# The second block's norms by token and the convolution's first tap on ScalarE, in a two-block fp32 kernel

## The chip, the cores and the metric

The kernel runs on one core of one Trainium2 chip, as one program. The metric is the device time of one execution in microseconds, over several runs; one further execution was taken with the hardware profiler, and all durations below are from it. Engines: PE is TensorE (its records of weight loads are PEld), DVE is VectorE, ACT is ScalarE, POOL is GpSimd, SP is SyncE.

## The reference, cut to what matters

Two blocks run on 256 tokens of width 2048, in fp32. The change is in the second one. Its input projection gives, for every token, q and k (12 heads each) and v (24 heads) of 128 columns, a gate z, and the queries of a cross attention. What the change touches is how these are made ready:

```python
def rms_norm(x, g):
    xf = x.astype(jnp.float32)
    y = xf * lax.rsqrt(jnp.mean(xf * xf, axis=-1, keepdims=True) + EPS)
    return (y * g.astype(jnp.float32)).astype(x.dtype)

def l2_norm(x):
    return (xf * lax.rsqrt(jnp.sum(xf * xf, axis=-1, keepdims=True) + EPS)).astype(x.dtype)
...
    qkv = jax.nn.silu(causal_depthwise_conv(p[..., :c_qkv], conv_w))      # DN_CONV = 4 taps
    q = l2_norm(q heads), k = l2_norm(k heads)                            # 24 heads of 128
...
    q = rms_norm(xq.reshape(B, S, XA_HEADS, XA_DIM), qn_g)                # cross attention: 4 heads of 256
    k = rms_norm(kv[..., :XA_WIDTH].reshape(B, -1, XA_HEADS, XA_DIM), kn_g)
```

## The kernel before

Data lie with features on the 128 partitions and the 256 tokens in the free dimension. The second block projects 88 tiles of 128 columns: eight for the cross attention's queries, then 40 pairs of tiles, numbered q from 0, that are q and k (pairs 0 to 11), v and z. A pair is seven groups of eight 128x128x128 products (one Strassen step), 56 in all; an fp32 product stands in the trace as two records. PE issues all of them from one line (L2263, in `halves`), and they are the filler of everything else in the block: `plan` lists the places of the program and how much filler goes behind each (a unit there is 7/4 products), and `fill(name)` issues it. The places that matter are n0 and n1 ahead of the cross attention, s, t and o of its four heads, j3, j4 and v0 behind it, and then six groups g0 to g5 of the recurrence. PE, ACT and DVE each run their own queue in order; ACT and DVE put their part of the pairs where `keeps_by`, `firsts_by` and `seconds_by` say, which compare a pair's groups with the filler's positions.

For each pair ACT copies two banks out after the second group (`keep`, L2503). DVE makes two sums behind the fourth group (`first`, L2720 and L2722) and the next pair's weight sums (L2702 to L2705), and the last sums behind the seventh group (`second`, L2733). Then `conv` runs the four taps of two tiles on DVE: the first as a product with a column (L2751), three as multiply-adds (L2754); ACT applies silu (L2510) into `A2`. The products of pair q wait for `first` of pair q-1 at their first group, for `second` of pair q-1 at the third, and for `keep` of pair q at the fifth.

There are five norms n = 0 to 4: n = 0 for the memory's keys, n = 1 for the cross attention's queries (groups of two tiles), n = 2, 3, 4 for eight tiles of q and k each. Each has four steps. ACT squares eight tiles (`norm_squares`, L2529). PE sums over the partitions with a matrix of ones as the stationary operand (`norm_sums`, L2288), which leaves the sum of each token and head on all 128 partitions. ACT takes the root of that (`norm_roots`, L2537), 128x1024 for n = 0 and 1, 128x2048 for the others. DVE takes the inverse of the same size (L2784) and multiplies (`norm_scale`, L2787, or L2790 with a gain). In DVE's queue the inverse of norms 1, 3 and 4 stands ahead of a `first`, and that of norm 2 ahead of the fourth head's row maxima.

Of the kernel before, what the change touches and what calls it, by code (L numbers as in the profile page):

```python
# [21 lines left out]
ALU = mybir.AluOpType  # L22
# [77 lines left out]
def build(nc, a, out):  # L100
# [30 lines left out]
    with outer:  # L131
# [1930 lines left out]
        tmpa, keep2 = x_f[0:VH, 0:TX], x_f[0:VH, TX:2 * TX]  # L2062
        sqj = o_f[:, 0:2048].rearrange("p (t n) -> p t n", n=TX)
# [57 lines left out]
        with phase() as c:  # L2121
            (x1_ready, x1_out, x1_back, group_done, kept, paired, xsums, tsums, hin, ab_done, ab_out, tile_done, conv_chain, silu_done, z_silu, gated, xq_taken,
             squares, summed, roots, inverse, normed, bchain, gchain, dchain2, mchain, ttr, tout, s_done, mx, e_done, rcp,
# [6 lines left out]
                "z_silu", "gated", "xq_taken", "qk_squares", "qk_summed", "qk_roots", "qk_inverse", "qk_normed",  # L2130
# [7 lines left out]
            with nc.Block() as block:  # L2138
# [81 lines left out]
                def _(pe):  # L2220
# [59 lines left out]

                    def norm_sums(n):
                        per = norm_jobs[n][1]
                        pe.wait_ge(squares, n + 1)
                        if n:
                            pe.wait_ge(roots, n)
# [28 lines left out]
                    norm_sums(1)  # L2314
                    fill("n1")
                    for h in range(XH):
# [12 lines left out]
                        if h == 2:  # L2329
                            norm_sums(2)  # L2330
# [17 lines left out]
                        fill(f"o{h}")  # L2348
                    fill("j3")
                    norm_sums(3)  # L2350
                    fill("j4")
                    norm_sums(4)
                    fill("v0")
                    for i in range(NG):
                        if i == 0:
                            pe.wait_ge(roots, 5)
                            pe.wait_ge(xo_out, XH)
# [124 lines left out]
                def _(act):  # L2482
                    at = [0]
# [21 lines left out]
                    def silu(q):  # L2505
                        kind, _, dst, had = pair_tiles(q)
                        to = pair_to[:, q % 2, :, :]
                        if kind == "c":
                            act.wait_ge(conv_chain, DCONV * (had + 2))
# [5 lines left out]
                    def pairs_to(upto, whole=False):  # L2515

                        for q in range(at[0], upto):
                            keep(q)
                            if q:
                                silu(q - 1)  # L2520
                            at[0] = q + 1

                    def drain(name, then):
                        pairs_to(keeps_by(name, then))
# [6 lines left out]
                    def norm_roots(n):  # L2531
# [51 lines left out]
                    drain("n0", "n1")  # L2583
                    norm_roots(1)
                    drain("n1", "s0")
                    for h in range(XH):
# [5 lines left out]
                        drain(f"s{h}", f"t{h}")  # L2592
                        act.wait_ge(pt_done, h + 1)
# [11 lines left out]
                        if h == 2:  # L2605
                            norm_roots(2)
# [5 lines left out]
                    drain("j4", "v0")  # L2612
# [8 lines left out]
                    drain("v0", "g0a")  # L2621
# [50 lines left out]
                    pairs_to(NQ)  # L2672
# [3 lines left out]
                def _(dve):  # L2676
# [63 lines left out]
                    def conv(q):  # L2740
                        _, wt, _, had = pair_tiles(q)
                        if had >= 4:
                            dve.wait_ge(silu_done, had - 2)
                        dve.wait_ge(paired, 4 * q + 4)
                        for d in range(DCONV):
                            for j in range(2):
# [3 lines left out]
                                if d == 0:  # L2750
                                    ins = nc.vector.tensor_scalar(to, src, tap, None, ALU.mult)  # L2751
                                else:
                                    dve.wait_ge(conv_chain, DCONV * had + 2 * (d - 1) + j + 1)
                                    ins = nc.vector.scalar_tensor_tensor(to[:, d:], src[:, 0:TX - d], tap, to[:, d:],  # L2754
                                                                         ALU.mult, ALU.add)
                                ins.then_inc(conv_chain, 1)
# [22 lines left out]

                    def norm_scale(n):  # L2780
                        x, per, _, gain = norm_jobs[n]
                        w = 8 // per
                        dve.wait_ge(roots, n + 1)
                        nc.vector.reciprocal(rtj[:, 0:w, :], rtj[:, 0:w, :]).then_inc(inverse, 1)  # L2784
                        dve.wait_ge(inverse, n + 1)
                        if gain is None:
                            nc.vector.tensor_tensor(x, x, rtj[:, :, :], ALU.mult).then_inc(normed, 1)  # L2787
                        else:
                            for t in range(8):
                                nc.vector.scalar_tensor_tensor(x[:, t, :], x[:, t, :], pcol(gain, t % 2), rtj[:, t // 2, :],  # L2790
                                                               ALU.mult, ALU.mult).then_inc(normed, 1)
# [11 lines left out]
                    for m in range(MT):  # L2803
                        nc.vector.tensor_scalar(x1[:, m, :], y_tok[:, m, :], ssf[:, SCALE1, m:m + 1], None, ALU.mult).then_inc(x1_ready, 1)
                    norm_scale(0)
# [15 lines left out]
                    drain("n0", "n1")  # L2821
# [237 lines left out]
```

## Time and profile before

| what | us |
|---|---|
| median of 3 runs | 3817.94 |
| lowest and highest | 3814.05, 3818.92 |
| the profiled execution's own time | 3816.08 |
| its span | 3814.4 |
| in it, the first product of pair 0 to the end of v0 | 301.5 of the span |
| in it, the recurrence and the last filler | 600.9 of the span |

The span begins with the first instruction of the profile and ends with the last; some 1.7 us of the execution lie around it. The page's first section gives busy times over the whole span, but the block that the change is in covers less than a third of it, so the rows of the section below are of that block's stretches. An idle time in a row is put down to the instruction that released the engine. PEclk is the share of TensorE's full clock that was granted in a stretch.

### The profile page before, as it was taken

The page shows a single profiled execution, that of the slowest core. Times are in us where ns is not written, and L with a number is a line of the kernel's source. Part 1 is how long each engine was busy: PE and PEld are TensorE (multiplying, and loading weights), DVE is VectorE, ACT ScalarE, POOL GpSimd, SP SyncE. Part 2 cuts the span into 40 slices and gives each one's busy share as a digit, 9 for nine tenths or more (in the row PEclk, how much of TensorE's full clock was granted, in tenths as well). Part 3 has the DMA queues.
Part 4 walks back from the last instruction along what each step waited for, and adds up shares of the span by engine and source line. Part 5 has one row for each costly group of instructions (what it writes and reads, how often), then busy time and mean ns, then how long its engine had stood idle before and what let it go on. Part 6 is the DMA issues. An engine that isn't in the chain of part 4 may idle for free. (4 is left out here: it accounts for less than half of the span.)

```text
span 3814.4 us, 50735 instructions
## 1 busy us (share of the span) xinstructions
PE 3604.1 (94%) x20578; PEld 3176.4 (83%) x20578; DVE 2113.4 (55%) x4109; ACT 626.1 (16%) x1423; POOL 927.4 (24%) x813
## 2 busy tenths in 40 slices
PE   8999999999999999998778999999878899999899
PEld 6878887899988888887667777776878899999888
DVE  5882102255520789655787444445366867666554
ACT  0002112100011122220446000002121122222100
POOL 0001000101000344546776545453000121122000
PEclk9999999999999999999999999999989999999999
DMA  5434332344544799997994999997323322221342
GB/s 211 143 130 144 144 122 78 122 177 168 219 188 167 262 364 385 385 388 241 313 316 175 347 334 330 346 336 265 122 101 132 111 95 95 95 95 67 129 192 111
DMA packets 159013, 776.64 MB, mean 204 GB/s; under 512 B 19476, under 2 KB 21420, under 8 KB 122812
## 3 DMA queue, kind: packets, MB, share of 16 engines
q1 hardware_dynamic: 100536, 518.52, 37.2%
q0 software_dynamic: 57344, 251.69, 18.0%
q10 hardware_dynamic: 900, 3.17, 0.3%
q8 instruction: 164, 2.69, 0.3%
q14 instruction: 69, 0.57, 0.0%
HBM read 762.67 MB, written 10.64 MB: 203 GB/s over the span
## 5 line engine op out<-in xcount | busy, mean ns | idle before, releaser
L405 PE MATMUL PS<-mem,ring 128*128 128x272 f32 (+1 forms) x2816 | 647.7, 393 | 3.0 <-DMA ring<-in_first_tiles 3.0
L405 PEld LDWEIGHTS PS<-mem,ring 128*128 128x128 f32 x2816 | 541.6, 193 | 106.9 <-issue 4.6
L1272 POOL DMA_INDIRECT mem<-in_peer_ug,idx x256 | 313.0, 1223 | 639.7 <-DVE idx L1786 347.1
L1839 DVE CUSTOM_DVE_ANT_0 mem<-mem 128x1152 f32<-128x1152 f32 x256 | 349.0, 1365 | 137.4 <-DMA mem<-in_peer_ug,idx 131.2
L1924 DVE SCALAR_TENSOR_TENSOR mem<-mem 128x768 f32<-128x768 f32 x256 | 261.3, 1021 | 288.0 <-DMA mem<-in_peer_vg,idx 282.1
L1386 PE MATMUL PS<-mem 128*128 128x256 f32 x1792 | 387.5, 379 | 1.4 <-DMA mem<-in_peer_ud 1.4
L2263 PE MATMUL PS<-mem,ring 128*128 128x128 f32 x2560 | 328.1, 283 | 60.8 <-DVE mem L2722 42.4
L1386 PEld LDWEIGHTS PS<-mem 128*128 128x128 f32 x1792 | 340.2, 190 | 48.3 <-DMA mem<-in_peer_ud 2.2
L2263 PEld LDWEIGHTS PS<-mem,ring 128*128 128x128 f32 x2560 | 312.4, 199 | 64.3 <-issue 45.0
L413 PEld LDWEIGHTS PS<-mem,ring 128*128 128x128 f32 x3136 | 350.3, 192 | 0.1
L413 PE MATMUL PS<-mem,ring 128*128 128x128 f32 x3136 | 350.3, 275 | 0.0
L1298 POOL DMA_INDIRECT mem<-in_peer_vg,idx x256 | 278.7, 1089 | 280.4 <-DVE mem L1924 224.2
L2216 POOL TENSOR_TENSOR mem<-mem,ring 128x512 f32<-128x512 f32 x84 | 114.2, 1376 | 769.8 <-DVE mem L2874 573.4
L1462 PE MATMUL PS<-mem,ring 128*128 128x512 f32 (+1 forms) x768 | 297.4, 523 | 2.1 <-DMA mem<-in_peer_vd 2.1
L1462 PE MATMUL PS<-mem 128*128 128x512 f32 (+1 forms) x768 | 296.2, 523 | 0.0
L1462 PEld LDWEIGHTS PS<-mem,ring 128*128 128x128 f32 x768 | 217.9, 298 | 71.0 <-DMA mem<-in_peer_vd 2.7
L1462 PEld LDWEIGHTS PS<-mem 128*128 128x128 f32 x768 | 217.7, 298 | 68.4
L2263 PE MATMUL PS<-mem 128*128 128x128 f32 x1920 | 240.4, 278 | 11.9 <-DVE ring L2733 11.9
L2263 PEld LDWEIGHTS PS<-mem 128*128 128x128 f32 x1920 | 228.4, 194 | 13.4 <-DVE ring L2733 13.0
L934 DVE SCALAR_TENSOR_TENSOR mem<-mem 128x256 f32<-128x256 f32 x480 | 191.7, 473 | 0.0
L1425 PE MATMUL PS<-mem 128*128 128x256 f32 x512 | 131.5, 403 | 44.6 <-DMA mem<-in_mem_w_kv 43.6
L1425 PEld LDWEIGHTS PS<-mem 128*128 128x128 f32 x512 | 97.2, 200 | 65.4 <-DMA mem<-in_mem_w_kv 47.4
(407 smaller groups left out, 4414.4 us busy)
## 6 DMA issues: line engine op xcount, KB each, us to landing
ring<-in_first_tiles SPq DMA_DIRECT2D x144, 1024.0 KB, 4.8
ring<-in_dn_tiles SPq DMA_DIRECT2D x88, 1024.0 KB, 4.9
mem<-in_peer_vd SPq DMA_DIRECT2D x128, 640.0 KB, 7.0
mem<-in_peer_ud SPq DMA_DIRECT2D x128, 448.0 KB, 6.6
ring<-in_out_panels SPq DMA_DIRECT2D x16, 2048.0 KB, 8.5
ring<-in_w_out SPq DMA_DIRECT2D x8, 2048.0 KB, 8.9
ring<-in_peer_wq SPq DMA_DIRECT2D x8, 2048.0 KB, 8.0
mem<-second_keys SPq DMA_DIRECT2D x64, 256.0 KB, 5.3
```

Of the source, the lines that this page charges most:

```text
L405: last = nc.tensor.matmul(PS[:, 4 + n % 4, 0:T if wide else TX], wslots[slot_of[n]][:, k, :], x, start=(k == 0), stop=(k == KT - 1))
L413: last = nc.tensor.matmul(PS[:, bank, at * P:(at + 1) * P], w[:, k, :], x[:, k, :], start=(k == 0), stop=(k == KH2 - 1))
L934: ins = nc.vector.scalar_tensor_tensor(dst, src, w, acc[:, j % 4, :], ALU.mult, ALU.add)
L1272: nc.gpsimd.indirect_dma_start(Ug[:, at % US, :], None, a["peer_ug"], bass.IndirectOffsetOnAxis(ap=idx[:, n, j:j + 1], axis=0)).then_inc(u ...
L1298: nc.gpsimd.indirect_dma_start(Vg[:, at % GS, :], None, a["peer_vg"], bass.IndirectOffsetOnAxis(ap=idx[:, n, j:j + 1], axis=0)).then_inc(v ...
L1386: last = nc.tensor.matmul(PS[:, i % BANKS_U, 0:TX], Ut[i % UT][:, k * P:(k + 1) * P], xnD[:, k, :], start=(k == 0), stop=(k == KU - 1))
L1425: last = nc.tensor.matmul(PS[:, KVB[side], 0:PW], x, y, start=(k == 0), stop=(k == KT - 1))
L1462: last = nc.tensor.matmul(to, weights_of[m][:, i // LO, :, i % LO], Vd[:, i % VS, at:at + w], start=(i == 0), stop=(i == NKEY - 1))
L1839: nc.vector.tensor_tensor_reduce(out=Ug[:, at % US, :], in0=Ug[:, at % US, :], in1=h_tok[:, m, CU:D], scale=1.0, scalar=0.0, op0=ALU.mult, ...
L1924: nc.vector.scalar_tensor_tensor(hc, Vg[:, at % GS, :], dots[:, m, h * PTOP + j:h * PTOP + j + 1], hc, ALU.mult, ALU.add).then_inc(vg_used, 1)
L2216: nc.gpsimd.tensor_tensor(No[:, m, :, :], NT_[:, m, :, :], lev[:, l:l + 1, :].broadcast_to([P, VG, P]), ALU.mult).then_inc(no_ready, 1)
L2263: ins = nc.tensor.matmul(to, w[:, k, :], y[:, k, :], start=(k == 0 and group in (0, 2, 3)), stop=(k == GROUP - 1), skip_group_check=True)
```

## The change

Norms 1 to 4 no longer put each token's sum on all partitions. `token_sums` makes the squares the stationary operand and one column of ones the moving one, so the sums of a norm stand as 128 tokens by 8 or 16 columns. Root (ACT) and inverse (DVE, the new `norm_inverse`) work on that small tile, `per_token`. `spread_inverse` brings the inverses back to all partitions with 8 or 16 products against the identity, into four PSUM banks, and DVE multiplies from there. The filler is divided so that a norm's sums, inverse and spread stand apart, and 16 units of it move from v0 to n1. In `conv` the first tap is left out; ACT makes it as a copy scaled by a column (`first_tap`) behind a pair's last sums, and DVE's remaining three taps wait for it (`tapped`). Norm 0, the other matrices and all data are as before.

```diff
-        plan = [("x0", 128), ("n0", 24), ("n1", 40)]
+        plan = [("x0", 128), ("n0", 24), ("n1a", 8), ("n1b", 20), ("n1c", 28)]
...
-        plan += [("j3", 24), ("j4", 120), ("v0", 112)]
+        plan += [("j3", 24), ("j4a", 8), ("j4b", 24), ("j4c", 88), ("v0a", 8), ("v0b", 24), ("v0c", 64)]
...
+        per_token = o_f[:, 2048:2064]
+        spread_of = PS[:, 0:4, :].rearrange("p b (t n) -> p (b t) n", n=TX)
...
+                    def token_sums(n):
...
+                        for g in range(8 // per):
+                            for m in range(MT):
+                                for e in range(per):
+                                    last = nc.tensor.matmul(PS[:, 0, g * MT + m:g * MT + m + 1],
+                                                            sqj[:, g * per + e, m * P:(m + 1) * P], ones[:, 0:1],
+                                                            start=(e == 0), stop=(e == per - 1))
...
+                    def spread_inverse(n):
...
+                        pe.wait_ge(inverse, n + 1)
+                        for g in range(8 // per):
+                            for m in range(MT):
+                                c = g * MT + m
+                                last = nc.tensor.matmul(spread_of[:, g, m * P:(m + 1) * P],
+                                                        per_token[:, c:c + 1].broadcast_to([P, P]), ident[:, :],
+                                                        start=True, stop=True)
...
-                    norm_sums(1)
-                    fill("n1")
+                    token_sums(1)
+                    fill("n1a")
+                    fill("n1b")
+                    spread_inverse(1)
+                    fill("n1c")
...
-                            norm_sums(2)
+                            token_sums(2)
...
                         fill(f"o{h}")
+                        if h == 2:
+                            spread_inverse(2)
...
+                    def first_tap(q):
...
+                            act.wait_ge(paired, 4 * q + 4)
+                            for j in range(2):
+                                tap = PD * (CQKV // P) + wt + j
+                                nc.scalar.activation(dacc[:, had % 4 + j, :], pair_to[:, q % 2, 2 * j:2 * j + 2, :].rearrange("p b n -> p (b n)"),
+                                                     ACT.Copy, scale=dcw[:, tap:tap + 1]).then_inc(tapped, 1)
...
-                        nc.scalar.activation(rtj[:, 0:w, :], PS[:, 0:w // 2, :].rearrange("p b (t n) -> p (b t) n", n=TX),
-                                             ACT.Sqrt, bias=eps_c[:, :], scale=scale).then_inc(roots, 1)
+                            nc.scalar.activation(per_token[:, 0:MT * w], PS[:, 0, 0:MT * w], ACT.Sqrt, bias=eps_c[:, :],
+                                                 scale=scale).then_inc(roots, 1)
...
-                        for d in range(DCONV):
+                        for d in range(1, DCONV):
...
+                                if d == 1:
+                                    dve.wait_ge(tapped, had + j + 1)
...
                         if gain is None:
-                            nc.vector.tensor_tensor(x, x, rtj[:, :, :], ALU.mult).then_inc(normed, 1)
+                            nc.vector.tensor_tensor(x, x, by, ALU.mult).then_inc(normed, 1)
```

In the orders below L2265 is the line of the pairs' products after the change (L2263 before). PE's queue around norm 3 before, with the sums on all partitions as L2288:

```order
L2263 MATMUL PS<-mem 128x128 x2
L2288 MATMUL PS<-mem,ones 128x256 x8
L2263 MATMUL PS<-mem 128x128 x6
L2263 MATMUL PS<-mem,ring 128x128 x24
L2263 MATMUL PS<-mem 128x128 x16
```

PE's queue around norm 3 after, with `token_sums` as L2294 and `spread_inverse` as L2306; pair 10 begins with the last 14 of the 22 products ahead of L2306:

```order
L2265 MATMUL PS<-mem,ring 128x128 x22
L2294 MATMUL PS<-ones,mem 128x1 x16
L2265 MATMUL PS<-mem,ring 128x128 x2
L2265 MATMUL PS<-mem 128x128 x16
L2265 MATMUL PS<-mem,ring 128x128 x8
L2265 MATMUL PS<-mem 128x128 x8
L2265 MATMUL PS<-mem,ring 128x128 x22
L2306 MATMUL PS<-ident,mem 128x128 x16
L2265 MATMUL PS<-mem,ring 128x128 x2
L2265 MATMUL PS<-mem 128x128 x16
```

The sums move half a pair later, and the spread stands 56 products behind them and two products ahead of the third group of pair 10.

DVE's queue at the same norm before: inverse and multiplication stand directly ahead of a `first`.

```order
L2754 SCALAR_TENSOR_TENSOR ring<-ring,dcw 128x253 x2
L2784 RECIPROCAL mem<-mem 128x2048
L2787 TENSOR_TENSOR mem<-mem 128x2048
L2720 TENSOR_TENSOR mem<-PS,mem 128x128
L2722 TENSOR_TENSOR mem<-PS,mem 128x128
L2702 TENSOR_TENSOR mem<-ring 128x1024
```

DVE's queue there after, with the inverse as L2839, the multiplication as L2849, `first` as L2778 and L2780, `second` as L2791:

```order
L2839 RECIPROCAL mem<-mem 128x16
L2778 TENSOR_TENSOR mem<-PS,mem 128x128
L2780 TENSOR_TENSOR mem<-PS,mem 128x128
L2760 TENSOR_TENSOR mem<-ring 128x1024
L2761 TENSOR_TENSOR ring<-ring 128x1024
L2763 TENSOR_TENSOR mem<-ring,mem 128x1024
L2784 TENSOR_TENSOR ring<-mem 128x128
L2849 TENSOR_TENSOR mem<-mem,PS 128x2048
L2791 TENSOR_TENSOR ring<-PS,mem 128x384
```

The inverse is now ahead of `first` of pair 9 and the multiplication between it and `second` of pair 9. At norm 4 the multiplication stands directly behind the inverse and ahead of `first` of pair 13; at norm 2 both stand ahead of the fourth head's row maxima, as before.

ACT's queue at norm 3 after, with the squares as L2581, the root as L2589, the first taps as L2560 and `keep` as L2542; before, a `keep` came directly behind the root:

```order
L2581 ACTIVATE mem<-mem 128x2048
L2589 ACT_TABLE_LOAD
L2589 ACTIVATE mem<-PS,eps_c 128x16
L2560 ACTIVATE ring<-ring,dcw 128x256 x2
L2542 ACTIVATE mem<-PS 128x2x128
L2549 ACT_TABLE_LOAD
```

The first taps of pair 8 now wait behind the root of norm 3, and the `keep` of pair 9 behind them.

## Rows read from the trace of the kernel before

**Rows 1.** Windows: stretch, its length, busy us (records) of PE PEld DVE ACT POOL, PEclk, DMA.

```profile
2711.70:3013.20 301.50, 243.60 (x1938) 238.01 (x1939) 200.39 (x298) 64.20 (x90) 0.00 (x0) 0.90 0.31 113
3013.20:3614.10 600.90, 565.87 (x4909) 559.21 (x4907) 397.75 (x599) 144.03 (x234) 114.19 (x84) 0.99 0.25 91
```

**Rows 2.** Waits of PE from 2711 to 3014.9: us in total, times, longest.

```profile
PE PS L2263 <- DVE mem L2722: 38.9, 5, 14.9
PE PS L2263 <- ACT mem L2503: 17.6, 2, 15.9
PE PS L2288 <- ACT mem L2529: 1.1, 1, 1.1
```

**Rows 3.** Timeline of PE at norm 3: start, us, line, records, idle time before.

```profile
2882.34 3.62 PE L2288 MATMUL PS<-mem,ones 128*128 128x256 f32 x16
...
2903.95 6.41 PE L2263 MATMUL PS<-mem,ring 128*128 128x128 f32 x32 [14.87 <-DVE mem L2722]
2910.19 3.74 PE L2263 MATMUL PS<-mem 128*128 128x128 f32 x32
```

**Rows 4.** Timeline of DVE at norm 2.

```profile
2832.72 12.95 DVE L2784 RECIPROCAL mem<-mem 128x2048 f32<-128x2048 f32 x1 [8.08 <-ACT mem L2537]
2845.71 2.29 DVE L2787 TENSOR_TENSOR mem<-mem 128x2048 f32<-128x2048 f32 x1
2847.91 0.42 DVE L2828 TENSOR_REDUCE mem<-PS 128x1 f32<-128x256 f32 x1
...
2848.89 0.15 DVE L2830 TENSOR_SCALAR mem<-mem 128x1 f32<-128x1 f32 x1
2850.40 0.29 DVE L2720 TENSOR_TENSOR mem<-PS,mem 128x128 f32<-128x128 f32 x1 [1.36 <-ACT mem L2503]
```

**Rows 5.** Timeline of PE at its other waits in this stretch.

```profile
2736.54 6.48 PE L2263 MATMUL PS<-mem,ring 128*128 128x128 f32 x32 [8.58 <-DVE mem L2722]
...
2755.55 2.02 PE L2263 MATMUL PS<-mem,ring 128*128 128x128 f32 x16 [1.86 <-DVE mem L2722]
...
2776.98 1.89 PE L2324 MATMUL PS<-mem 128*128 128x256 f32 x8
2778.71 1.05 PE L2263 MATMUL PS<-mem 128*128 128x128 f32 x8
2781.42 2.05 PE L2263 MATMUL PS<-mem,ring 128*128 128x128 f32 x16 [1.66 <-ACT mem L2503]
...
2805.64 5.46 PE L2263 MATMUL PS<-mem,ring 128*128 128x128 f32 x32 [1.86 <-DVE mem L2722]
...
2850.42 3.78 PE L2263 MATMUL PS<-mem,ring 128*128 128x128 f32 x16 [15.90 <-ACT mem L2503]
...
2973.35 5.87 PE L2263 MATMUL PS<-mem,ring 128*128 128x128 f32 x32 [11.74 <-DVE mem L2722]
```

**Rows 6.** Timeline of PE in the recurrence: products with 64 moving columns.

```profile
3136.79 1.05 PE L2395 MATMUL PS<-mem 128*128 128x64 f32 x8
3137.68 1.05 PE L2391 MATMUL PS<-mem 128*128 128x64 f32 x8
```

**Rows 7.** Windows in the first block: 64 records of 16 columns, 32 behind them, 32 elsewhere.

```profile
561.51:567.75 6.24, 6.24 (x65) 6.09 (x65) 0.00 (x0) 0.38 (x1) 0.00 (x0) 0.74 0.48 168
567.75:576.57 8.82, 8.82 (x33) 7.21 (x33) 0.86 (x8) 0.00 (x0) 0.00 (x0) 0.80 0.01 2
...
637.00:644.00 7.00, 7.00 (x34) 5.96 (x33) 2.72 (x4) 0.00 (x0) 0.00 (x0) 1.00 0.00 1
```

**Rows 8.** Groups by line: count, busy us, mean ns, idle time before.

```profile
L1523 ACT ACTIVATE mem<-mem 128x256 f32<-128x256 f32 x16 | 6.6, 425 | 26.4 <-DVE mem L1711 26.4
L1570 ACT ACTIVATE mem<-mem 128x16 f32<-128x16 f32 x16 | 4.4, 274 | 0.0
L2751 DVE TENSOR_SCALAR ring<-ring,dcw 128x256 f32<-128x256 f32 x48 | 16.6, 387 | 0.0
```

**Rows 9.** Timeline of PE in the recurrence's third group, at the second level.

```profile
3232.58 1.38 PE L2263 MATMUL PS<-mem 128*128 128x128 f32 x10 [1.51 <-DVE ring L2733]
```

More of the change, by code:

```diff
@@ L2121, in build @@
         with phase() as c:
-            (x1_ready, x1_out, x1_back, group_done, kept, paired, xsums, tsums, hin, ab_done, ab_out, tile_done, conv_chain, silu_done, z_silu, gated, xq_taken,
-             squares, summed, roots, inverse, normed, bchain, gchain, dchain2, mchain, ttr, tout, s_done, mx, e_done, rcp,
+            (x1_ready, x1_out, x1_back, group_done, kept, paired, xsums, tsums, hin, ab_done, ab_out, tile_done, conv_chain, silu_done, z_silu, tapped, gated, xq_taken,
+             squares, summed, roots, inverse, spread, normed, bchain, gchain, dchain2, mchain, ttr, tout, s_done, mx, e_done, rcp,
              p_ready, pt_done, pt_out, xo_done, xo_out, copied, decay_out, kqk_done, d_ready, dec_ready,
@@ L2279, in fill @@
                             at[1] += 1
+                    def token_sums(n):
+                        per = norm_jobs[n][1]
+                        pe.wait_ge(squares, n + 1)
+                        if n == 1:
+                            pe.wait_ge(roots, 1)
+                        else:
+                            pe.wait_ge(normed, 14 + n)
+                        for g in range(8 // per):
[4 more added lines that the diff above has]
+                                                            start=(e == 0), stop=(e == per - 1))
+                        last.then_inc(summed, 1)
+                    def spread_inverse(n):
+                        per = norm_jobs[n][1]
+                        pe.wait_ge(inverse, n + 1)
[5 more added lines that the diff above has]
+                                                        start=True, stop=True)
+                        last.then_inc(spread, 1)
                     def norm_sums(n):
@@ L2513, in silu, with pairs_to @@
                             nc.scalar.activation(to, to, ACT.Silu).then_inc(z_silu, 2)
[L2515 to L2521, printed above, removed]
+                    def first_tap(q):
+                        kind, wt, _, had = pair_tiles(q)
+                        if kind == "c":
+                            act.wait_ge(paired, 4 * q + 4)
[3 more added lines that the diff above has]
+                                                     ACT.Copy, scale=dcw[:, tap:tap + 1]).then_inc(tapped, 1)
+                    def pairs_to(upto, taps=0):
+                        while at[0] < upto or at[1] < taps:
+                            if at[0] > at[1]:
+                                first_tap(at[1])
+                                at[1] += 1
+                            else:
+                                keep(at[0])
+                                if at[0]:
+                                    silu(at[0] - 1)
+                                at[0] += 1
                     def drain(name, then):
-                        pairs_to(keeps_by(name, then))
+                        pairs_to(keeps_by(name, then), seconds_by(name, then))
                     def norm_squares(n):
@@ L2592, in _ @@
                         drain(f"s{h}", f"t{h}")
+                        if h == 2:
+                            norm_roots(2)
                         act.wait_ge(pt_done, h + 1)
```

94 lines of the change are left out of this document (57 added, 37 removed).

## The prediction, made before the run

> **What bounds the kernel now.** I looked first for the engine that sets the end. PE carries the whole span; the question is only where it waits. The table of windows by stage [rows 1] shows it: from pair 0 to the end of v0 PE is busy 243.6 of 301.5 us at a granted clock of 0.90, while in the recurrence behind it PE is busy 565.9 of 600.9 at 0.99. So the stretch with the norms holds 58 us of idle PE and a lower clock, and the recurrence has little to give. The list of PE's waits in that stretch [rows 2] names what ends them: 38.9 us for L2722 (`first` on DVE), 17.6 for L2503 (`keep` on ACT), 1.1 for the squares; 57.6 in all. The timelines show why. At norm 2 DVE spends 12.95 us on the inverse of 128x2048 and 2.29 on the multiplication, and the row maxima and `first` stand behind them [rows 4]; PE gets on 15.9 us late. At norms 3 and 4 PE waits 14.87 and 11.74 for the `first` behind an inverse, at norm 1 (half the size) 8.58 [rows 3, 5]. These four are 51.1 of the 57.6; three waits of 1.66 to 1.86 us at the cross attention's heads and some crumbs are the rest [rows 5]. After a wait PE is also slow for a while: 32 records take 3.74 us at full clock, but 6.48, 5.46, 6.41 and 5.87 behind four of the waits, and 16 records 3.78 where half of 3.74 is 1.87, behind the fifth [rows 3, 5]. That is 2.7 + 1.7 + 2.7 + 2.1 + 1.9 = 11.1 us at the lower of the two clocks. So waits and clock together hold 68.7 us.
>
> **What the change does, part by part.**
>
> *The inverses.* 6.5 + 3 x 12.95 = 45.4 us leave DVE's queue (norm 1 counted as half of 12.95 [rows 4]). The new inverse is 128x16 at most: above the 0.15 of the 128x1 row and below the 0.42 of a 128x256 one [rows 4]; I take 0.2. The root falls from 128x2048 to 128x16, 0.27 by L1570 [rows 8]. With hand-overs root and inverse need about 1 us, and PE has 32 to 56 products (7 to 12.5 us) between a norm's sums and its spread, so the spread finds its inverse ready. Two queues have to be looked at for that. On ACT nothing that waits stands ahead of a root. On DVE norm 3's and norm 4's inverses stand behind a convolution whose first taps, on ACT, now stand behind that same root: 2 x 0.42 for the taps [rows 8] and six multiply-adds of under 0.5 each, 4 to 5 us in all, still inside 12.5. So that delay costs nothing as long as the 12.5 us stand there; without them it would show as 4 us on PE.
>
> *What PE gets instead.* The 56 spread products (8 + 3 x 16) are 112 records. A 128x128 product runs at 0.111 us a record, and one with 64 moving columns too: 8 records from 3136.79 to 3137.68 [rows 6]. So 112 x 0.1116 = 12.5 us, all on PE's path. The stationary operand is one column repeated, which no row shows; the lower bound is the 0.1116 of the same size, the upper one a doubled load, 0.22, or 12.5 us more. I take the lower, since the load is of the same size. The 64 sums with one moving column are 128 records; since 64 columns cost what 128 cost, I take 0.1116, 14.3 us, against four old sums of 3.5 (16 records, 3.62 [rows 3]): 0.4 more. Their lower bound is the mean of the products with 16 moving columns and weights of 16 to 128, 6.24 / 65 at a clock of 0.74, so 0.071 [rows 7], or 5.2 us less. Together PE gets 12.9 us more.
>
> *Which waits stay.* The places are read from the new order. A head's scores that fall half a pair in make PE wait for a `keep` behind the exponentials, those that fall on a pair's boundary for a `first` behind the row maxima; the 28 products that move ahead only exchange the two kinds. Heads 0 and 2 are now of the first kind, 1.66 each, head 1 of the second, 1.86 and a little [rows 5]: 5.4. At head 3 DVE multiplies only once the spread is done: 2.29, row maxima 1.13 (from 2847.91 to 2849.04), two additions of 0.29 [rows 4], 0.25 of hand-overs, less the 1.73 of the scores on PE [rows 5]: 2.5. At norm 3 the multiplication stands ahead of `second` of pair 9, which pair 10 needs two products after the spread: 2.29 + 0.55 (128x384, carried on from 0.29 for 128 and 0.42 for 256) + 0.2 - 0.45 = 2.6. At norm 4 it stands ahead of `first` of pair 13, needed at once: 2.29 + 0.6 + 0.2 = 3.1. With 0.2 at head 2's transposes (a `keep` behind the root) 13.8 us stay of 57.6. Norm 1's multiplication ends just before pair 2 needs the `first` behind it, so nothing is left there.
>
> *The clock.* Six waits of 1.7 to 3.1 us: the rows have no loss at two such waits and 1.7 at the third, and up to 2.7 at the long ones [rows 5]; I take 5, with 0 and 13 as ends. The sums with one moving column are new to the clock. The nearest rows are 64 records of 16 columns: the granted clock was 0.74 in that burst, 0.80 in the 32 records behind it, which took 8.82 us where the same number takes 7.0 at 1.00 [rows 7]. That burst lost 1.5 and 1.8 us. A burst here has half as many records; I take 1.7 each, 6.8 for the four, with 0 and 13 as ends. Together 11.8 against the 11.1 of before.
>
> *The first tap.* 48 operations of 0.387 us leave DVE, 48 of about 0.42 go to ACT [rows 8]. Between 2711 and 3013 ACT is busy 64 of 301 us and DVE 200 [rows 1], and in the plain pairs PE does not wait for either, so I cost this at nothing there; DVE's next weight sum (over 1 us) covers the taps. Behind a tap on ACT stands the `keep` of the next pair, which PE needs only after 32 products, 7.1 us into that pair; the tap can start about 1 us into it. In the recurrence the taps now stand ahead of the second level's copies on ACT and wait for the same `second` that PE waits 1.51 us for [rows 9]; by that the copy comes some 0.3 us too late in three groups of six, 0.9 us lost, and about 0.5 is gained where a `conv` held PE. Net 0.4 lost.
>
> The Trainium skill's page "ScalarE: Activation LUTs", section "Rules for kernel authors", puts a plain multiplication on VectorE, not on ScalarE, which speaks against this part. The rows agree that an operation is dearer on ACT (0.425 against 0.387); by that rule the sum would lose 48 x 0.04 = 1.8 us, if ACT were on the path, but the engine with time to spare is ACT.
>
> **The sum.** 57.6 - 13.8 = 43.8 of waits, less 12.9 of new PE work, less 0.7 of clock, less 0.4: 29.8 us off. The profiled execution took 3816.08, so 3786.3; its time lies 1.9 below the median of the runs, 3817.94, and inside their spread, so I put the median at 3787.
>
> **The rivals.**
>
> *Narrow sums at the low clock.* If each burst of one-column sums drops the clock to 1.2 GHz during and behind itself, and the short waits do so too, the clock loses 26 instead of 11.8: 3801. For it: the burst with 16 columns lost 3.3 us [rows 7]. Against it: it is half as long here. The Trainium skill's page "TensorE: Matmul & The Clock Gate", Part 1, says that throttled is the default and activity lifts it; rows 7 agree that the clock fell with few moving columns, and no run here shows it for one.
>
> *A new wait in place of the old.* If the multiplication, which now waits for the spread, holds more of DVE's queue than I see (its weight sums and `second` behind a late `first`), norms 2, 3 and 4 each cost twice what I counted and norm 1 some 3: 11 more, 3798. Against it: at 2755.55 a late `first` cost only its own 1.86 [rows 5].
>
> *Slower than before.* The spread's stationary operand is one column read 128 times. If such a load is not as fast as a plain one, its price falls 112 times on PE's path. It decides from 0.45 us a record, four times a plain one ((29.8 + 7.6) / 112 = 0.33 on top); at eight times the kernel would take 3874. Nothing in the rows shows such a load, so I give it little.
>
> *The stalls are not DVE's.* If the weights' transfers held the pairs and the inverses only hid them, nothing would change. Against it: PE ran the pairs behind each inverse without a wait for a transfer in the list of waits [rows 2].
>
> **How the numbers follow.** The forecast, with its clock terms anywhere between their ends: 0.81, from 3772 to 3800. Narrow sums with short waits at their worst 0.08, a new wait 0.04, a slow load from the point where it decides 0.04, no change 0.03. The range of 3771 to 3802 covers the first three cases nearly whole, and leaves some 0.12 out. What a measurement of this kernel can tell from no change is about 0.2%, 7.6 us. Faster by more: 0.93; within it: 0.03; slower by more: 0.04, nearly all of it the slow load.
>
> **What would show it.** In the changed profile: the inverses under 0.3 us; 112 records of the spread at 0.11 us each; PE's waits in the stretch at 12 to 16 us, none over 4, with the largest at norm 4 and norm 3; the stretch 270 to 275 us long; clock about 0.9. Spread products waiting for an inverse would make the cover wrong, records over 0.2 us the price of the spread, a granted clock under 0.85 the clock term, and PE waiting for `tapped` work in the plain pairs the part on the taps.

## The result, and the profile after

The changed kernel took 3787.98 us (median of 8 runs, 3775.39 to 3797.19) against 3815.02 (8 runs, 3807.01 to 3818.92): a ratio of 0.9933, 95% interval 0.9915 to 0.9951. Its profiled execution took 3787.53 us with a span of 3785.8. The forecast of 3787 held, but its two stages were off by more than 4 us each, in opposite directions, and that it was met to within 1 us is luck:

| stage, us in the profiled executions | before | after | predicted difference | measured |
|---|---|---|---|---|
| up to the first product of pair 0 | 2711.8 | 2713.3 | 0 | +1.5 |
| from there to the first product of the recurrence ("the stretch" below) | 303.0 | 268.2 | -30.2 | -34.8 |
| from there to the last pair's last product ("the recurrence") | 592.9 | 597.8 | +0.4 | +4.9 |
| the rest | 206.7 | 206.5 | 0 | -0.2 |

The same two windows of before and, below them, of after, with columns as in [rows 1]. Their limits are each kernel's own first products, so they differ a little from the limits in [rows 1]:

```profile
2711.80:3014.80 303.00, 245.17 (x1953) 239.55 (x1954) 201.98 (x300) 64.10 (x89) 0.00 (x0) 0.90 0.32 114
3014.80:3607.70 592.90, 564.22 (x4894) 557.55 (x4892) 390.79 (x594) 143.40 (x233) 114.19 (x84) 0.99 0.24 87
```

```profile
2713.30:2981.50 268.20, 254.85 (x2129) 251.07 (x2130) 149.72 (x271) 73.07 (x122) 0.00 (x0) 0.97 0.36 129
2981.50:3579.30 597.80, 568.00 (x4894) 561.06 (x4892) 384.22 (x577) 149.70 (x249) 114.20 (x84) 0.98 0.24 86
```

In the stretch PE is busy 9.7 us longer and idle 44.5 us less; DVE's busy time falls by 52 us. In the recurrence PE has the same 4894 records and is busy 3.8 us longer with them. The waits of PE in the stretch after, which answer to [rows 2]:

```profile
PE PS L2265 <- DVE mem L2780: 7.2, 3, 3.0
PE PS L2265 <- ACT mem L2542: 3.3, 2, 1.7
PE PS L2265 <- DVE ring L2791: 2.4, 1, 2.4
PE PS L2265 <- issue: 0.6, 1, 0.6
PE PS L2265 <- DVE ring L2761: 0.3, 2, 0.2
```

13.2 us without the 0.6 at the start, against 57.8 (the 57.6 of [rows 2] and 0.2 for a weight sum). PE at norm 3 after, which answers to [rows 3] (sums L2294, spread L2306):

```profile
2868.72 4.86 PE L2294 MATMUL PS<-ones,mem 128*128 128x1 f32 x32
2873.43 1.20 PE L2265 MATMUL PS<-mem,ring 128*128 128x128 f32 x4
2874.43 5.30 PE L2265 MATMUL PS<-mem 128*128 128x128 f32 x32
...
2888.06 3.74 PE L2306 MATMUL PS<-ident,mem 128*128 128x128 f32 x32
2891.63 0.61 PE L2265 MATMUL PS<-mem,ring 128*128 128x128 f32 x4
2894.64 5.47 PE L2265 MATMUL PS<-mem 128*128 128x128 f32 x32 [2.40 <-DVE ring L2791]
```

The wait of 14.87 is one of 2.40 now. The 32 spread records take 3.57 us from start to start (2888.06 to 2891.63), 0.112 each. But the sums take 4.71 and the 36 records behind them 6.14, where full clock gives 3.49 (norm 4's sums) and 4.02. DVE at the same norm, as [rows 4] for norm 2: three taps of two tiles, the inverse, and later the multiplication and `second`:

```profile
2874.31 2.46 DVE L2809 SCALAR_TENSOR_TENSOR ring<-ring,dcw 128x255 f32<-128x255 f32 x6 [6.83 <-ACT ring L2560]
2876.68 0.25 DVE L2839 RECIPROCAL mem<-mem 128x16 f32<-128x16 f32 x1
...
2891.83 2.29 DVE L2849 TENSOR_TENSOR mem<-mem,PS 128x2048 f32<-128x2048 f32 x1 [7.77 <-PE PS L2306]
2894.03 0.55 DVE L2791 TENSOR_TENSOR ring<-PS,mem 128x384 f32<-128x384 f32 x1
```

The inverse takes 0.25 and is ready 11 us ahead of the spread; DVE waits 6.83 for the first tap on ACT, and nobody waits for DVE there.

### The profile page after: what moved, and what is told of

The parts are those of the page before. It is cut to its first block and busy times, and to the rows that moved or that the text cites. A ratio compares the mean times of both kernels' runs of the same rounds, so it can differ in the third digit from the quotient of the medians.

```text
span 3785.8 us, 51066 instructions
## 1 busy us (share of the span) xinstructions
PE 3626.0 (96%) x20754; PEld 3200.3 (85%) x20754; DVE 2053.8 (54%) x4061; ACT 641.7 (17%) x1472; POOL 925.4 (24%) x813
## 5 line engine op out<-in xcount | busy, mean ns | idle before, releaser
L2265 PE MATMUL PS<-mem,ring 128*128 128x128 f32 x2560 | 320.7, 278 | 16.2 <-DVE mem L2780 11.9
L2265 PEld LDWEIGHTS PS<-mem,ring 128*128 128x128 f32 x2560 | 304.5, 194 | 19.7 <-issue 14.4
L2265 PE MATMUL PS<-mem 128*128 128x128 f32 x1920 | 244.6, 281 | 14.3 <-DVE ring L2791 14.3
L2265 PEld LDWEIGHTS PS<-mem 128*128 128x128 f32 x1920 | 232.1, 197 | 15.8 <-DVE ring L2791 15.6
```

The costliest lines, as they stand in the source:

```text
L2265: ins = nc.tensor.matmul(to, w[:, k, :], y[:, k, :], start=(k == 0 and group in (0, 2, 3)), stop=(k == GROUP - 1), skip_group_check=True)
```

## The experiments

The part ahead of pair 0 is the same in all kernels and took 2705.8 to 2724.3 us in the fourteen profiles, which is most of the scatter of the times: the two profiles of the changed kernel differ by 11.4 us in their span and by 11.0 in this part. So kernels are compared by the two stages, with the ratio to the kernel before beside them. What each label stands for is told with its experiment below. A loss at the lower clock is the time from a row's start to the next row's start, less the next row's wait, less its records at full clock (0.1117 us, or 0.2155 with 256 columns).

| kernel | ratio, 95% interval | stretch | PE waits in it | lost in and behind sums | lost behind waits | recurrence |
|---|---|---|---|---|---|---|
| before | 1 | 303.0 | 57.8 | 0 | 11.4 | 592.9 |
| after | 0.9933, 0.9915 to 0.9951 | 268.2 | 13.2 | 4.8 | 3.3 | 597.8 |
| after_again | 0.9926, 0.9903 to 0.9948 | 266.3 | 13.2 | 1.7 | 4.6 | 600.5 |
| tap_back | 0.9903, 0.9887 to 0.9920 | 264.7 | 13.2 | 1.7 | 3.0 | 595.3 |
| tap_only | 1.0023, 1.0011 to 1.0034 | 300.3 | 57.4 | 0 | 8.7 | 603.3 |
| tap_late | 0.9919, 0.9904 to 0.9934 | 268.3 | 13.2 | 4.9 | 3.3 | 591.4 |
| wide_sums | 0.9908, 0.9890 to 0.9927 | 264.7 | 13.1 | 0 | 5.1 | 598.0 |
| late_mul | 0.9906, 0.9881 to 0.9932 | 260.4 | 7.3 | 6.5 | 0 | 600.0 |
| late_mul_tap_back | 0.9901, 0.9885 to 0.9917 | 262.0 | 7.3 | 8.2 | 0 | 593.5 |
| late_wide_act | 0.9881, 0.9862 to 0.9899 | 253.9 | 7.3 | 0 | 0 | 592.2 |
| late_wide_dve | 0.9885, 0.9866 to 0.9904 | 255.1 | 7.2 | 0 | 1.7 | 595.3 |
| spread_twice | 0.9969, 0.9955 to 0.9982 | 279.0 | 13.2 | 3.3 | 3.2 | 595.2 |
| no_cover | 0.9936, 0.9915 to 0.9956 | 267.2 | 14.6 | 1.4 | 4.2 | 602.6 |
| short_inverse | 0.9877, 0.9855 to 0.9898 | 252.3 | 14.6 | 0 | 3.4 | 592.9 |

**Was it the inverse?** In short_inverse the kernel before keeps every instruction, but the inverse of norms 1 to 4 covers 16 columns or 8, and the root is taken of a constant, so that nothing grows without bound; the inverses of the other columns are left out, and its norms are not the reference's:

```diff
-                                              ACT.Sqrt, bias=eps_c[:, :], scale=scale).then_inc(roots, 1)
+                                              ACT.Sqrt, bias=eps_c[:, :], scale=scale if n == 0 else 0.0).then_inc(roots, 1)
...
-                        nc.vector.reciprocal(rtj[:, 0:w, :], rtj[:, 0:w, :]).then_inc(inverse, 1)
+                        to = rtj[:, 0:w, :] if n == 0 else rtj[:, 0, 0:2 * w]
+                        nc.vector.reciprocal(to, to).then_inc(inverse, 1)
```

> The kernel before with the inverse of norms 1 to 4 taken over 128x16 only (128x8 at norm 1), all else in place: sums, root, multiplication, first tap on DVE. Left out: the inverse of the other columns, and the root is taken of a constant, so the norms' factors are not the reference's. Theory (the inverse's 12.95 and 6.5 us of DVE are what PE waited for): the waits of 8.58, 15.90, 14.87 and 11.74 fall to about 2.3, 3.2, 2.2 and 0, PE's waits in the stretch from 57.6 to 12 to 16, the stretch from 303.0 to 250 to 256, 0.986 to 0.989 of the kernel before. Rival (the root on ScalarE or the multiplication holds PE as well): waits over 25 us, stretch over 265.

PE's waits in its stretch:

```profile
PE PS L2263 <- DVE mem L2722: 8.1, 4, 2.2
PE PS L2263 <- ACT mem L2503: 4.9, 2, 3.2
PE PS L2288 <- ACT mem L2529: 1.1, 1, 1.1
...
```

57.8 us became 14.6, the stretch 252.3, as the theory said; the waits at norms 1 to 3 are 2.23, 3.21 and 2.17, and norm 4's is gone. So 43.2 us of the waits were the inverse's; what the root of 128x2048 and the multiplication, both still in place, can have held is inside the 2 to 3 us left at a norm. It also shows what there was to gain in this order if the short inverse cost PE nothing: 3766.2 us, 0.9877.

**What do the spread and its cover cost?** spread_twice issues each spread product twice:

```diff
-                        for g in range(8 // per):
+                        for g in [g for _ in range(2) for g in range(8 // per)]:
```

> The changed kernel with every spread product issued twice, the second overwriting the first with the same values. Theory (the spread is on PE's path at the price of a plain product): 112 more records at 0.112 us, 12.5 us more in the stretch, which becomes 279 to 281, the waits behind it unchanged at 13.2. Rival (part of the spread lies in time in which PE would wait anyway): less than 8 us more, with shorter waits.

The stretch less the losses at the lower clock is 272.5, against 260.1 in the changed kernel: 12.4 us for 112 records, 0.111 each, with the waits unchanged. The spread is on PE's path at the price of a plain product. no_cover takes the filler between sums and spread away at norms 3 and 4:

```diff
-        plan += [("j3", 24), ("j4a", 8), ("j4b", 24), ("j4c", 88), ("v0a", 8), ("v0b", 24), ("v0c", 64)]
+        plan += [("j3", 24), ("j4a", 0), ("j4b", 0), ("j4c", 120), ("v0a", 0), ("v0b", 0), ("v0c", 96)]
```

> The changed kernel with the filler between sums and spread of norms 3 and 4 taken away (0 units in j4a, j4b, v0a and v0b, all of them in j4c and v0c). In the changed kernel the inverse of these norms was ready 3.5 us behind the last sum (2873.4 to 2876.9 and 2933.8 to 2937.3): the root, then the first taps behind it on ScalarE, the six multiply-adds on DVE that wait for these, then the inverse. Theory (the filler is the cover of that chain): PE waits 3.4 to 3.7 us for the inverse at each of the two, and the waits of 2.40 and 3.00 for the multiplication go, since it falls into the middle of a pair: stretch within 3 us of the changed kernel's 266 to 268. Rival (root and inverse alone are the chain): waits of 1 us or less for the inverse, stretch 260 to 263.

PE's waits in its stretch, and PE at norm 3:

```profile
PE PS L2306 <- DVE mem L2839: 6.8, 2, 3.4
PE PS L2265 <- DVE mem L2780: 4.2, 2, 2.3
...
```

```profile
2864.78 3.63 PE L2294 MATMUL PS<-ones,mem 128*128 128x1 f32 x32
2871.83 6.32 PE L2306 MATMUL PS<-ident,mem 128*128 128x128 f32 x32 [3.42 <-DVE mem L2839]
```

3.42 and 3.41 us for the inverse, at the low end of what was expected, and the waits of 2.40 and 3.00 for the multiplication are gone. The chain behind the sums is 3.4 us, and the 56 products hide it. But the stretch is as long without them (267.2 against 268.2 and 266.3): two waits for the inverse, 6.8 us, stand where two for the multiplication, 5.4, were. In this order the cover earned nothing that shows.

**Where do the last waits come from?** late_mul moves the multiplications of norms 2 to 4 behind a pair's last sums:

```diff
-        plan += [("j3", 24), ("j4a", 8), ("j4b", 24), ("j4c", 88), ("v0a", 8), ("v0b", 24), ("v0c", 64)]
+        plan += [("j3", 24), ("j4a", 8), ("j4b", 28), ("j4c", 84), ("v0a", 8), ("v0b", 36), ("v0c", 52)]
...
+                        if h == 3:
+                            norm_scale(2)
                         drain(f"t{h}", f"s{h + 1}" if h < XH - 1 else "j3")
-                        if h == 2:
-                            norm_scale(2)
```

> The changed kernel with the filler of j4b and v0b made longer by 4 and 12 units, taken from j4c and v0c, and norm 2's multiplication issued behind the fourth head's softmax, so that the multiplications of norms 2, 3 and 4 stand behind a pair's last sums and not ahead of a first or second that PE waits for. Theory: the waits of 2.40 (norm 3) and 3.00 (norm 4) go, the 2.32 at the fourth head falls to the 1.86 of the second, and 1.7 + 1.5 us at the lower clock behind the two go with them: 6 to 9 us faster than the changed kernel, 0.990 to 0.992 of the kernel before. Rival (the wait only moves to the next first): no gain on the changed kernel, PE's waits in the stretch stay above 11 us.

DVE at norm 3:

```profile
2878.81 2.45 DVE L2809 SCALAR_TENSOR_TENSOR ring<-ring,dcw 128x255 f32<-128x255 f32 x6
2885.47 2.29 DVE L2849 TENSOR_TENSOR mem<-mem,PS 128x2048 f32<-128x2048 f32 x1 [4.21 <-PE PS L2306]
2888.00 0.29 DVE L2778 TENSOR_TENSOR mem<-PS,mem 128x128 f32<-128x128 f32 x1 [0.24 <-PE PS L2265]
```

The multiplication now stands in a gap of DVE and ends before the `first` behind it has its products. 13.2 us of waits became 7.3, and nothing was lost behind them. The stretch fell by 5.9 to 7.8 us; 6.5 us at the lower clock remained, all in and behind the sums, the next question.

**Do one-column sums lower the clock?** In wide_sums the moving operand is 128 columns of ones, and the root reads every 128th column:

```diff
-                                    last = nc.tensor.matmul(PS[:, 0, g * MT + m:g * MT + m + 1],
-                                                            sqj[:, g * per + e, m * P:(m + 1) * P], ones[:, 0:1],
+                                    last = nc.tensor.matmul(spread_of[:, g, m * P:(m + 1) * P],
+                                                            sqj[:, g * per + e, m * P:(m + 1) * P], ones[:, :],
...
```

> The changed kernel with 128 columns of ones as the moving operand of the token sums in place of one; the root reads one column in 128. Same number of records, and by the products of 128 and of one column (0.112 and 0.109 us a record) about the same length: 0.4 us more for the four. Theory (one moving column lets the clock fall: 1.5 to 1.7 us lost behind norm 1's sums in all four profiles, 3.2 in and behind norm 3's in two of them): these losses go, PE is at full clock through and behind the sums, some 2 to 4 us faster than the changed kernel in the stretch (266.3 and 268.2 there). Rival (the clock falls for another reason): the same 1.5 us behind norm 1's sums stands again.

Windows of the changed kernel (the sums of norm 3, the 36 records behind them, the sums of norm 4), then of wide_sums (norm 3's sums and what is behind them):

```profile
2868.72:2873.43 4.71, 4.71 (x34) 4.71 (x33) 0.00 (x0) 0.00 (x0) 0.00 (x0) 0.73 0.44 174
2873.43:2879.57 6.14, 6.14 (x38) 6.14 (x38) 2.62 (x7) 3.36 (x6) 0.00 (x0) 0.65 0.00 0
...
2930.32:2933.81 3.49, 3.49 (x34) 3.49 (x33) 1.69 (x2) 0.00 (x0) 0.00 (x0) 1.00 0.92 373
```

```profile
2879.40:2882.97 3.57, 3.57 (x34) 3.57 (x33) 0.00 (x0) 0.00 (x0) 0.00 (x0) 1.00 0.58 227
2882.97:2886.99 4.02, 4.02 (x38) 4.02 (x37) 2.62 (x7) 1.92 (x5) 0.00 (x0) 1.00 0.00 0
```

By its records PE is busy all through both, and the clock falls to 0.73 and 0.65 with one moving column and stays at 1.00 with 128. In the eight profiles with one-column sums, 14 of 32 bursts lost 1.4 to 3.3 us (norm 1 in seven, norm 3 in five, norm 4 in two, norm 2 never); in the three with wide sums none of 12 did. So the narrow product is the cause: its moving operand and, with that, its output of one column (the wide sums also fill four PSUM banks instead of a corner of one, which no run separates). Whether it bites goes with the burst's place in the program and differs between runs of one kernel; why norm 2 is spared stays open. The stretch is 1.6 to 3.5 us shorter than in the two profiles of the changed kernel, although 5.1 were lost behind waits; the intervals of the two times overlap.

**What does the first tap cost?** tap_back undoes it in the changed kernel, as the diff shows, and leaves `first_tap` out of ACT's queue; tap_only does it alone in the kernel before, the same lines the other way round.

```diff
-                        for d in range(1, DCONV):
+                        for d in range(DCONV):
...
-                                if d == 1:
-                                    dve.wait_ge(tapped, had + j + 1)
+                                if d == 0:
+                                    ins = nc.vector.tensor_scalar(to, src, tap, None, ALU.mult)
```

> The changed norms with the first tap on DVE as before. Theory (the norms are the whole gain, the tap is worth nothing): 0.992 to 0.995 of the kernel before, within 0.2% of the changed kernel; PE's waits from pair 0 to the end of v0 stay at 13 us, give or take 1, and in the recurrence fall from 29.4 us to the 28.7 of before. Rival (the tap's 48 x 0.387 = 18.6 us of DVE are part of the gain): waits in the stretch grow by 5 to 10 us, the kernel is at 0.995 to 0.997.

> The kernel before with the first tap alone moved to ScalarE; norms and filler as before. Theory (tap worth nothing): 0.999 to 1.001, the long waits of 8.6 to 15.9 us unchanged or each some 1 us longer, where the tap now stands behind the root of 128x2048 on ScalarE and the inverse behind the convolution. Rival (DVE's load is the bound): 5 to 10 us faster, 0.9975 to 0.9985.

tap_only is slower than before by 0.23%, 4 to 13 us, and tap_back is at 0.9903 where the changed kernel is at 0.9926 beside it (these two intervals overlap), so both theory and rival failed: the tap on ACT is not free and no gain, it costs. In the stretch it changes no wait (13.2 either way), and PE's waits in the recurrence, which were to fall, are 29.9 in tap_back against 29.4. The cost is in the recurrence: 599.6 on average in the seven profiles with the tap as the change has it (595.2 to 603.3), 593.4 in the seven others (591.4 to 595.3). PE at a group's second level, in the changed kernel and in tap_back:

```profile
3097.78 1.16 PE L2421 MATMUL PS<-mem 128*128 128x128 f32 x8 [0.85 <-POOL mem L2218]
3098.78 1.06 PE L2265 MATMUL PS<-mem,ring 128*128 128x128 f32 x8
3101.35 1.38 PE L2265 MATMUL PS<-mem 128*128 128x128 f32 x10 [1.51 <-DVE ring L2791]
3102.86 1.82 PE L2430 MATMUL PS<-mem 128*128 128x64 f32 x8
3104.48 1.91 PE L2434 MATMUL PS<-mem 128*128 128x64 f32 x8
```

```profile
3193.78 1.38 PE L2265 MATMUL PS<-mem 128*128 128x128 f32 x10 [1.51 <-DVE ring L2778]
3195.00 1.00 PE L2430 MATMUL PS<-mem 128*128 128x64 f32 x8
3195.84 1.05 PE L2434 MATMUL PS<-mem 128*128 128x64 f32 x8
```

From the ten products to the next row 1.51 us pass in one and 1.22 in the other: a pause of 0.3, which no wait in the list names. ACT at this place in the changed kernel makes the taps (L2560) first and the second level's copies (L2709) behind them:

```profile
3101.33 0.91 ACT L2560 ACTIVATE ring<-ring,dcw 128x256 f32<-128x256 f32 x2 [7.56 <-DVE ring L2791]
3102.14 1.06 ACT L2709 ACTIVATE mem<-PS 128x512 f32<-128x512 f32 x2
```

Behind the pause the rows of eight take 1.62 to 1.71 instead of 0.84 to 0.90, and the granted clock from there to the full rows is

```profile
3101.35:3111.84 10.49, 10.36 (x53) 10.20 (x53) 6.19 (x12) 1.85 (x4) 0.00 (x0) 0.58 0.01 2
```

that is, most of 10 us at 1.2 GHz, a loss of 5.3 us with the pause; the same rows lose 0.4 to 0.5 where the pause stands and the clock holds, so the clock's part is 4.9. In the seven profiles with the tap ahead of the copy this pause (0.2 or 0.3) stands 24 times and such a loss behind eight of them; in the seven others the wait of 1.51 stands 22 times at this place, without the pause and without such a loss. tap_late tests it by order alone: ACT makes the copies first, then the taps.

```diff
                                 nc.scalar.activation(Pb[:, m, :, :], q4(m), ACT.Copy).then_inc(p_out, 1)
-                            drain(f"g{i}p{l}", f"g{i}p{l + 1}" if l < LEV - 1 else f"g{i}c0")
+                            if l == 1:
+                                pairs_to(0, late)
+                            name, then = f"g{i}p{l}", f"g{i}p{l + 1}" if l < LEV - 1 else f"g{i}c0"
+                            late = seconds_by(name, then)
+                            if l or keeps_by(name, then) > at[0]:
+                                pairs_to(keeps_by(name, then), late)
```

> The changed kernel with one change on ScalarE in the recurrence: the first taps that stood ahead of a group's second copies stand behind them. In the profiles with the tap on ScalarE the recurrence took 597.8, 600.5, 600.0 and 603.3 us, with it on DVE 592.9 and 595.3. Theory (the taps hold the copies, PE pauses 0.3 us more right behind three other waits, and falls to the lower clock there, 5 us each time): the ten products behind the wait of 1.51 take 1.2 us again and not 1.5, the 5 us losses behind them go, recurrence 592 to 596, 4 to 6 us faster than the changed kernel. Rival (the losses are chance, or come from something else that the tap does): recurrence 597 or more with losses of 5 us behind the wait of 1.51, time as the changed kernel.

ACT and PE at the same place in tap_late:

```profile
3102.13 0.60 ACT L2709 ACTIVATE mem<-PS 128x512 f32<-128x512 f32 x1 [1.41 <-PE PS L2421]
3104.48 0.91 ACT L2560 ACTIVATE ring<-ring,dcw 128x256 f32<-128x256 f32 x2 [1.75 <-DVE ring L2796]
```

```profile
3104.50 1.38 PE L2265 MATMUL PS<-mem 128*128 128x128 f32 x10 [1.51 <-DVE ring L2796]
3105.72 1.00 PE L2430 MATMUL PS<-mem 128*128 128x64 f32 x8
```

1.22 us again, no loss of 5 us, and a recurrence of 591.4. The cost of the tap is its place in ACT's queue. The times can't be told apart (0.9919 against 0.9933 and 0.9926, with overlapping intervals); the stage decides, here and in late_wide_act below, which has the same order and a recurrence of 592.2.

**All together, and the changed kernel again.**

> Both edits of the first four runs that made the changed kernel faster: the multiplications behind a pair's last sums, and the first tap on DVE. If the two are separate (the one in the stretch from pair 0 to the end of v0, the other mostly in the recurrence): that stretch 258 to 261 us (303.0 before, 260.4 with the late multiplications alone), the recurrence 592 to 596 (592.9 and 595.3 in the two profiles with the tap on DVE), so 40 us off in these two stages and 0.988 to 0.990 of the kernel before. Rival (the tap on DVE delays what the late multiplications had freed): waits come back in the stretch, over 10 us, and the kernel is no faster than either edit alone, 0.990 or above.

The waits are 7.3 and the recurrence 593.5, as expected, but 8.2 us were lost in and behind the one-column sums, so the stretch (262.0) and the ratio are a little above what was expected. With wide sums:

> The changed kernel with three edits that were run singly: multiplications behind a pair's last sums, 128 columns of ones in the token sums, and the first taps behind the second copies in the recurrence. If each does what it did alone: from pair 0 to the end of v0 254 to 257 us (260.4 with the late multiplications, of which 6.5 were lost at the lower clock in and behind the one-column sums), recurrence 591 to 595 (591.4 with the taps behind the copies). Some 48 us off these two stages, 0.986 to 0.989 of the kernel before. Rival (without the losses behind the sums the clock falls elsewhere): stretch 259 or more.

> The same with the first tap on DVE in place of the reordered one on ScalarE. If the tap on ScalarE cost time only by its place ahead of the copies, the two are alike: stretch 254 to 257, recurrence 592 to 596, 0.986 to 0.989, within 0.1% of the other. If it is worth its 18.6 us of DVE somewhere, this one is slower by 3 us or more.

```profile
2715.20:2969.10 253.90, 246.41 (x2129) 242.98 (x2130) 149.90 (x270) 73.19 (x122) 0.00 (x0) 1.00 0.38 136
2969.10:3561.30 592.20, 561.24 (x4894) 554.58 (x4892) 384.93 (x577) 150.55 (x249) 114.42 (x84) 0.99 0.24 87
```

These are the windows of late_wide_act: clock 1.00 in the stretch, 49.1 us off it, and 0.9881 of the kernel before, the lowest ratio of the versions that compute the whole; its interval ends at 0.9899, below where the changed kernel's two begin (0.9915 and 0.9903). late_wide_dve is at 0.9885: put in the right place, the tap on ACT is worth nothing that shows.

> The changed kernel once more, beside the others of its chip. In its first profile PE waited 13.2 us in the stretch from pair 0 to the end of v0 (57.6 before) and ran below full clock there by 8.1 us in all (11.3 before): 1.5 behind the one-column sums of norm 1, 3.3 in and behind those of norm 3, 3.3 behind the two longest waits. Theory: the waits come back to within 0.5 us, since they follow from the order; the places of the low clock may differ. If the one-column sums themselves lower the clock, the same 4.8 us stand again at norms 1 and 3. Time 0.991 to 0.995 of the kernel before.

The waits came back to the tenth. Of the losses, norm 1's sums lost 1.7 (1.5 the first time), and norm 3's were spared.

## Why the prediction was right, and where it was not

*The waits* (13.8 predicted to stay, 13.2 measured). Place by place: heads 0 to 2 1.66, 1.86, 1.66 as said; head 3 2.32 for 2.5; norm 3 2.40 for 2.6; norm 4 3.00 for 3.1; only the 0.2 at head 2's transposes did not come, 0.3 for weight sums did. That the inverse was the cause is shown by short_inverse, that the cover hides 3.4 us (predicted: 4) by no_cover.

*The new PE work* (12.9 predicted). The spread is 12.5, as the 0.1116 of [rows 6] said. The one-column sums at full clock take what the old ones took (3.49 against 3.5), so 0.4 less than predicted; what they lose at the lower clock is counted next.

*The clock* (0.7 lost predicted, 3.3 gained in the first profile, 5.1 in the second). The mechanism was right and both sizes too large: 6.8 for the sums against 4.1 on average in eight profiles, 5 for the short waits against 3.3 and 4.6. (Of the burst in [rows 7], 6.24 us at 0.74 make 1.6 us lost, not the 1.5 read there.) Two signs named in advance failed with it: the clock in the stretch was to be about 0.9 and is 0.97, and the stretch was to last 270 to 275 us and lasts 268.2. The step behind that was to take the 0.90 of before as a mark of slow products. Much of it is the clock of an idle PE; in the wait at norm 3 before it was

```profile
2889.00:2903.90 14.90, 0.08 (x1) 0.00 (x0) 14.83 (x5) 0.00 (x0) 0.00 (x0) 0.61 0.33 131
```

The Trainium skill's page "TensorE: Matmul & The Clock Gate", Part 1, has the clock follow how busy PE has been. The idle row agrees. The sums of norm 3, which the profile has busy for 4.71 of 4.71 us at 0.73, do not, if busy means what it means in the profile; that it means the same in the page is not shown here.

*The first tap* (0.4 lost predicted, some 6 lost). The step "the copy comes some 0.3 us too late in three groups of six, 0.9 us lost" had the place and the pause right (1.51 against 1.22). What failed was to price it by the pause: it stands behind waits of 1.13, 0.85 and 1.51, and in eight of 24 cases PE fell to the lower clock there, for 4.9 us. A tap on ACT took 0.50 us, for the 0.42 said. "I cost this at nothing" in the plain pairs was right: PE's waits in the stretch are 13.2 with the tap on either engine. The 0.5 said to be gained where a `conv` held PE is not shown: PE waits 29.4 us in the recurrence with the tap on ACT, 29.9 in tap_back and 28.7 before.

The Trainium skill's page "ScalarE: Activation LUTs", section "Rules for kernel authors", wants a plain multiplication on VectorE. The prediction priced that rule at 1.8 us and set it aside, since ACT has time to spare. tap_back and tap_only side with the rule here; but late_wide_act and late_wide_dve are alike, so the order of ACT's queue cost the time and not the engine's rate.

So 3787 was met because the stretch gained 4.6 us more than the sum and the recurrence lost 4.5 more. The chance of "faster" rested on the waits, and there the sum was right by its mechanism and not by luck: 0.6 us off in all, each place within 0.3.

## What to carry to other kernels

Look for a slow operation (here an inverse over copies of the same numbers) not by its share of its engine but by what stands behind it in that engine's queue, and move its result's use into a gap: that took 6 to 8 us more off the stretch here for no work at all. Price a short pause by where it stands: behind other waits 0.3 us can cost 5 through the clock. A result that agrees with its forecast is to be compared stage by stage, since errors of opposite sign hide in the total.

## What the runs showed of the hardware that was not expected

- Products with one moving column take as long as those with 128 (0.109 and 0.112 us a record), and in 14 of 32 bursts of 32 records PE fell to the lower clock in or behind them although by its records it was never idle; with 128 columns in none of 12.
- Products whose stationary operand is one column read 128 times cost PE what plain ones do: 112 records added 12.4 us.
- The inverse of 128x16 takes 0.25 us, that of 128x2048 12.95 [rows 4], 5.7 times a multiplication of that size.
- In one level of the recurrence, a fourth short pause (0.2 or 0.3 us) behind waits of 1.13, 0.85 and 1.51 us was followed by 10 us mostly at the lower clock in eight of 24 cases; without the fourth, in none of 22.
